# A two-layer hybrid decoder trunk: at a block's first attention step, the logits and exponentials placed ahead of the row factors' spreading and eviction

## What is computed

```python
score = sum_h relu(q_idx k_idx) * w_idx            # indexer, per query
score = where(causal, score, NEG_INF)
_, sel = top_k(score, 256)                          # 256 keys per query
logits = q k[sel] * scale + rel_bias[t5_bucket(q_pos - sel)]
logits = where(dist >= 0, logits, NEG_INF)
p = softmax(logits)                                 # 8 heads, one shared key/value head of 64
out = p v[sel]
```

## Time and profile before

| what | value |
|---|---|
| runs | 2717.36, 2715.64, 2711.79 us; median 2715.64 |
| the profiled execution | 2709.55 us, span 2707.8 us, mean granted TensorE clock 0.977 |
| TensorE busy | 2575.2 us, 95% |
| VectorE busy | 1551.7 us, 57% |
| ScalarE busy | 1019.2 us, 38% |
| GpSimd busy | 1312.4 us, 48% |
| HBM | 84 GB/s over the span |

### The profile page before, as it was taken

One profiled execution on the slowest core, in us unless ns is written; L12 is line 12 of the kernel. 1 busy time (PEld: TensorE's weight loads), 2 busy tenths in 40 slices (PEclk: granted clock), 3 DMA queues, 4 the chain that ended last, 5 costly groups with the idle time before them and its releaser, 6 DMA issues. The chain is left out here.

```text
span 2707.8 us, 34637 instructions
## 1 busy us (share of the span) xinstructions
PE 2575.2 (95%) x13515; PEld 2025.7 (75%) x13515; DVE 1551.7 (57%) x2691; ACT 1019.2 (38%) x1478; POOL 1312.4 (48%) x818
## 2 busy tenths in 40 slices
PE   8899889989999999999999999998999999999998
PEld 6667656767777777777777887766777777888887
DVE  4768777789997225844331394668899922211112
ACT  5232354233444533324344422432434354322222
POOL 3332244454454464535555532543546446655654
PEclk9989999999999999999999999999999999999999
DMA  5242113122222163323222342222222215333332
GB/s 163 72 133 58 40 57 92 51 75 65 76 76 71 51 191 87 86 63 95 85 82 82 86 129 56 81 60 63 78 65 76 71 51 184 89 97 102 101 117 86
DMA packets 385666, 232.92 MB, mean 86 GB/s; under 512 B 29592, under 2 KB 371552, under 8 KB 383072
## 3 DMA queue, kind: packets, MB, share of 16 engines
q1 hardware_dynamic: 385136, 229.62, 28.7%
q10 hardware_dynamic: 368, 1.08, 0.1%
HBM read 213.88 MB, written 14.69 MB: 84 GB/s over the span
## 5 line engine op out<-in xcount | busy, mean ns | idle before, releaser
L709 POOL TENSOR_TENSOR w_lo<-w_raw,w_hi 128x1024 fp32r<-128x1024 f32 (+2 forms) x408 | 902.2, 2212 | 1244.1 <-ACT w_hi L820 1244.1
L1744 PE MATMUL psum<-h_hi,w_hi 128*128 128x512 f32 x1984 | 799.3, 403 | 18.1 <-DVE scratch L1250 7.9
L820 ACT ACTIVATE w_hi<-w_raw 128x1024 fp32r<-128x1024 f32 (+2 forms) x408 | 397.3, 974 | 1092.7 <-PE psum L1744 1050.6
L1744 PE MATMUL psum<-h_lo,w_hi 128*128 128x512 f32 x1984 | 767.0, 393 | 0.9 <-POOL h_lo L717 0.9
L1744 PE MATMUL psum<-h_hi,w_lo 128*128 128x512 f32 x1984 | 515.1, 390 | 0.0
L1744 PEld LDWEIGHTS psum<-h_hi,w_hi 128*128 128x128 f32 x1984 | 377.0, 190 | 130.7 <-issue 35.4
L1744 PEld LDWEIGHTS psum<-h_lo,w_hi 128*128 128x128 f32 x1984 | 375.9, 190 | 79.3 <-issue 2.0
L1744 PEld LDWEIGHTS psum<-h_hi,w_lo 128*128 128x128 f32 x1984 | 373.9, 188 | 76.7
L1344 DVE MAX8 top<-scores 128x8 f32<-128x512 f32 (+5 forms) x352 | 324.0, 920 | 6.7
L1346 DVE MATCH_REPLACE8 scores<-top,scores 128x512 f32<-128x512 f32 (+5 forms) x352 | 318.8, 906 | 0.0
L1744 PE MATMUL psum<-a_hi,w_hi 128*128 128x512 f32 x704 | 286.5, 407 | 18.4 <-ACT w_hi L820 8.3
(11 more groups left out here) (310 smaller groups left out, 2946.7 us busy)
## 6 DMA issues: line engine op xcount, KB each, us to landing
w_raw<-in_w_ffn_in_dram SPq DMA_DIRECT2D x176, 512.0 KB, 3.8
w_raw<-in_w_ffn_out_dram SPq DMA_DIRECT2D x96, 384.0 KB, 3.1
w_raw<-in_w_in_dram SPq DMA_DIRECT2D x68, 512.0 KB, 3.8
w_raw<-in_w_out_dram SPq DMA_DIRECT2D x32, 512.0 KB, 3.6
x_half<-xs SPq DMA_DIRECT2D x8, 1024.0 KB, 7.0
xs<-x_half SPq DMA_DIRECT2D x8, 1024.0 KB, 6.5
w_raw<-in_w_ffn_out_dram SPq DMA_DIRECT2D x32, 256.0 KB, 2.6
out_dram<-mixed SPq DMA_DIRECT2D x8, 512.0 KB, 3.6
```

What stands on the lines that cost most here:

```text
L709: eng.tensor_tensor(w_lo(u, n), w_raw[:, u % 3, 0:n], w_hi[:, u % 2, 0:n].bitcast(F32), ALU.subtract).then_inc(sems["weights_ready"], 1)
L820: act(w_hi[:, u % 2, 0:n], w_raw[:, u % 3, 0:n], ACTF.Copy).then_inc(sems["hi_ready"], 1)
L1744: return eng.matmul(out_, lhsT, rhs, start=start, stop=stop, skip_group_check=True)
```

## The change

On both engines a call moves inside its step. On ScalarE, `row_factors` (the eviction) goes from ahead of the step's exponentials to behind them. On TensorE, `row_factors` (the spreading) goes from ahead of the step's logits to behind them. VectorE, GpSimd and SyncE keep their instructions and their order. The attention ends (`attend_end`) keep theirs too.

```diff
             def attend(l, h, b, j, s):                     # ScalarE
                 ...
-                if j == 0 and not first:
-                    row_factors(at_)
                 for n, g in enumerate(at_.banks):
                     i = 2 * j + n
                     eng.wait_ge(sems["nmax_ready"], st.add("nmax_ready"))
                     act(at_.prob[:, n, 0:nk], bank(g, 0, nk), ACTF.Exp, scale=-1.0, bias=nmax[:, i:i + 1],
                         accum_out=rsum[:, i:i + 1]).then_inc(sems["p_ready"], 1)
+                if j == 0 and not first:
+                    row_factors(at_)

             def attend(l, h, b, j, s):                     # TensorE
                 ...
                 if s == 0:
                     if not first:
                         values(at_, *((b, j - at_.pairs) if j else (b - 1, PAIRS - at_.pairs)))
-                    if j == 0 and not first:
-                        row_factors(at_)
                     ...
                     for g in at_.banks:
                         leave(g, "p_ready")
+                    if j == 0 and not first:
+                        row_factors(at_)
```

## The result

The changed kernel takes 2726.22 us in the median of its seven runs (2719.20 to 2727.68), the kernel before 2715.64 in its seven beside them: a ratio of **1.004, 95% interval 1.0028 to 1.0052**. The change costs about 10.6 us, 0.4%. The profiled execution took 2727.68 us, 18.1 more than that of before. Not all of it is the change: the attention of the first layer begins with the maxima of block 0, at 320.44 us in the trace of before, and nothing ahead of them is moved, yet there the changed kernel is already 9.6 us late. A second profile of the same kernel (the run `again`) is 1.6 us late there. So the two traces are compared from that point on, as shifts of VectorE's same instruction.

What follows compares the result with a forecast made beforehand. VectorE sets the pace through ScalarE in two stretches, TensorE elsewhere. Terms -0.94 + 5.1 + 3.0 + 0.45 = +7.6 us, giving a median of 2723.2 us; range 2713.5 to 2728, the forecast's own 2720 to 2726.

Steps and rivals of the forecast that it cites:

- Part 3, VectorE's delay: Block 6, both layers: VectorE's normalising waits 2.5 us for the late eviction and the delay reaches TensorE; +5.1 us in all.
- Part 4, the clock: Behind block 6's copies wait, grown to 3.9 us, TensorE's clock falls; 1.5 us a layer, +3.0 us in all.
- The refund at the next wait: At 821.65 TensorE's wait would shrink by what TensorE lost, so the fall there may be milder: up to 1.2 us back.
- Part 3's bound, the table load: Block 6, ScalarE: a second table load, 1.3 us a layer above the 2.5, as upper bound; not expected.
- Part 1, TensorE's half: Logits ahead of the spreading fill TensorE's 0.47 us wait for the factors at block 7; -0.94 us over two layers.
- Part 5, block 5: Block 5: normalising starts 1.7 us later, covered by 1.95 us of VectorE idle time: 0, else up to 1 us a layer.
- Part 5, the projection window: First layer's blocks 1 to 3: the late eviction delays VectorE's normalising and the next maxima; +0.45 us, bounds -0.5 and +1.2.
- Rival A: VectorE's delay is carried, but the clock doesn't fall or the fall is refunded at 821.65; +4.6 us, 2720.2; chance 0.25.
- B: Block 6: the delay isn't carried, as the copies hang on ScalarE's own order; -0.5 us, 2715.1; chance 0.10.
- C: Earlier logits shorten block 5's wait by 1.1 us and the clock stays up; 8 us faster, 2707.6; chance 0.03.
- D: Block 5's cover fails too and its delay is carried; +2 us on the forecast, 2725 to 2728; chance 0.06.

Runs made afterwards that it cites:

- act_only: The kernel before with only ScalarE's half, the eviction behind the exponentials; TensorE as before. 2720.99 us, ratio 1.003 to the kernel before.
- act_b6: The kernel before with the eviction behind the exponentials at block 6 alone, in each layer; 2723.76 us, ratio 1.0028 to the kernel before.
- deferred: The changed kernel with VectorE's normalising of the block before moved behind the next search round; 2710.30 us, ratio 0.9994 to the kernel before.
- fill: The changed kernel with unread filler products in TensorE's idle time at block 6 and at blocks 2 and 3; 2719.59 us, ratio 1.0011 to the kernel before.
- pe_only: The kernel before with only TensorE's half, logits ahead of the spreading; ScalarE as before. 2710.04 us, ratio 0.9995 to the kernel before.
- combined: The kernel before with TensorE's half everywhere, ScalarE's half with deferred normalising only in the first layer's projection window; 2716.90 us, ratio 1.0005 to the kernel before.
- maxima_first: TensorE's half everywhere, ScalarE's with deferred normalising in the projection window, block 5's four search rounds behind pair 0's maxima; 2711.87 us, ratio 0.9986 to the kernel before.
- spread: TensorE's half everywhere, ScalarE's with deferred normalising in the projection window, block 5's four search rounds spread over later steps; 2710.30 us, ratio 1.000 to the kernel before.

## Why the prediction was right, and which term was not

The forecast was 2723.2 us in 2713.5 to 2728; the median is 2726.22, 3.0 above it and inside the range, though 0.2 above the forecast's own 2720 to 2726. Against the kernel before it said +7.6 and +10.6 came. By the steps:

- **Part 3, VectorE's delay** (2 x 2.5): right, to 0.05 us. L1366 waits 2.48 and 2.47. The path was the one named: product, Silu, copies, values product. `act_only`, `act_b6` and `deferred` show that this wait and nothing else starts it.
- **Part 4, the clock** (2 x 1.5): the fall came, at an idle time of 4.46 us where 3.9 was forecast (counted from block 6's first maxima, the values product starts 2.6 us later and TensorE comes to the wait 0.5 us earlier; the 0.5 has no cause shown). Of its loss VectorE felt 2.18 us, by the row at 810.13 (forecast: 2.2 from the earlier trace rows). `fill` puts it at 2.2 by another route. The refund at the next wait came too: 2.69 instead of 3.15 us, followed by a half-clock stretch of some 3.4 us instead of 6.8, 0.9 back of the 1.2 allowed, though not for the reason given, the shorter wait (last section). Net 2.3 - 0.9 = 1.4 a layer for 1.5: right in sum, with the 0.9 open in its cause. The rule of the Trainium skill that was weighed there ("TensorE: Matmul & The Clock Gate", HAM oscillation) held at 4.46 us.
- **Part 3's bound, the table load**: ScalarE's exponential at 782.32 again starts 1.29 us after its load at 781.03, as in 60 of the 99 loads of this trace, so the 2.66 us of the Trainium skill ("ScalarE: Activation LUTs", What ACT_TABLE_LOAD costs) doesn't appear there. No second load did either: before has 99 too.
- **Part 1, TensorE's half** (-0.94): -0.78 and -0.76, so -1.5. The wait of 0.47 us is gone as said, and from the values product to the next unit it takes 4.51 us (873.45 to 877.96) for 5.22 (857.71 to 862.93). Of the rest, 0.17 us is that the next products start 0.92 us behind the spreading's start, now that they are the unit's, where the logits started 1.09 behind it; why was not looked into.
- **Part 5, block 5**: its L1366 waits 1.55 us (forecast 1.7), the two idle times behind it absorb that (0.21 us is left at 696.00), and block 6 begins unshifted (-0.05). The cover held.
- **Part 5, the projection window** (+0.45, bound +1.2): this is **the term that was mis-sized**. P costs +2.3 and +3.0 in the two profiles, and act_only +3.6. What was left out of it is TensorE's clock, which the forecast weighed at block 6 and here, without a word, put at nothing.

TensorE in time in P of the changed kernel; VectorE at block 2 and ScalarE ahead of TensorE's third row; the windows of the changed kernel, then of before. Last the place of TensorE's third row in `deferred`, and that kernel's window:

```profile
370.01 1.53 PE L1744 MATMUL psum<-xs,vw 128*64 128x128 f32 x24 [1.51 <-ACT xs L1021]
374.95 2.74 PE L2064 MATMUL psum<-cst,xs 128*128 128x128 f32 x12 [1.92 <-ACT xs L1037]
...
388.80 3.62 PE L1744 MATMUL psum<-xs,vw 128*64 128x128 f32 x32 [1.82 <-ACT xs L1021]
```

```profile
368.42 0.69 DVE L1366 TENSOR_TENSOR mixed<-psum,area 128x512 f32<-128x512 f32 x1 [1.36 <-ACT area L1025]
...
386.15 0.61 ACT L1025 ACTIVATE area<-psum 128x512 f32<-128x512 f32 x1
386.62 1.59 ACT L1021 ACTIVATE xs<-psum 128x512 f32<-128x512 f32 x3
```

```profile
374.00:382.00 8.00, 6.38 (x38) 5.05 (x40) 5.62 (x17) 3.99 (x12) 2.88 (x6) 0.57 0.00 0
388.00:394.00 6.00, 5.20 (x40) 4.00 (x40) 0.49 (x1) 0.70 (x2) 0.26 (x1) 0.72 0.00 0
```

```profile
340.00:392.00 52.00, 40.73 (x316) 28.02 (x315) 33.26 (x86) 26.26 (x73) 18.43 (x31) 1.00 0.07 22
```

```profile
377.52 1.97 PE L1750 MATMUL psum<-xs,vw 128*64 128x128 f32 x32 [1.83 <-ACT xs L1021]
```

```profile
340.00:392.00 52.00, 41.05 (x319) 28.28 (x317) 34.51 (x86) 27.25 (x76) 19.41 (x32) 1.00 0.08 24
```

Three waits of TensorE grew. L1366 of block 2 waits 1.36 us, the maxima behind it are late by it, and TensorE's wait for the next exponentials (374.95) goes from 0.89 to 1.92 us. And the eviction, at 386.15 for instance, stands between the exponentials and the copies, as the forecast said: TensorE's wait for the copies goes from 1.02 to 1.51 at block 2 and from 1.34 to 1.82 at block 3. The clock fell behind the 1.92 and the 1.82; before, the window from 340 to 392 us ran at 1.00 throughout. The forecast looked for falls only where an idle time grew toward the 3.15 us it knew. Falls between 340 us, where the moved steps begin, and 395 us, by run: changed 2, again 2, act_only 1, fill 1; none in before, pe_only, deferred, act_b6, combined, maxima_first and spread. The wait of 1.8 us for the copies is in deferred, combined, maxima_first and spread as well, and there the clock stayed at 1.00. So the falls come with the late eviction and an undeferred L1366, and never without.

This table divides P. It is worked out from the profiles: how much later than before each kernel is at four marks, counted from block 0's second maxima.

| run | block 2, second maxima (364.36) | block 3, first (372.88) | block 3, second (381.57) | end of P (390.97) |
|---|---|---|---|---|
| changed | +0.14 | +0.73 | +2.86 | +2.85 |
| again | +0.13 | +0.96 | +3.06 | +3.05 |
| act_only | +1.52 | +1.51 | +3.54 | +3.54 |
| deferred | -0.98 | -1.50 | -0.97 | -0.96 |

combined, maxima_first and spread, which defer L1366 in P too, agree with deferred to 0.04 us. That row holds what the earlier logits bring less what the evictions cost ScalarE. Against it the changed kernel loses 1.1 us at block 2 to VectorE's wait, as `again` does. At block 2, then, the forecast was near: +0.43 was said, +0.14 came. At block 3 the changed kernel loses 1.1 and 1.6 us more and `again` 1.4 and 1.6, where the clock is down, so some 2.7 to 2.9 us go with the two falls. In act_only the one fall falls on the values product of block 3, which takes 3.51 us for 1.97: of the 2.03 us lost there 1.5 are the clock and 0.5 the eviction. `fill`, without the second fall, comes out 1.3 to 1.5 us under the changed kernel's two profiles. That act_only is the latest in P with only one fall has its reason in the first column: it lacks what the earlier logits bring.

With P at its measured +2.3 to +3.0 (from its first mark) and block 7 at -1.5, the forecast's sum would have been -1.5 + 5.1 + 3.0 + 2.3 to 3.0 = 8.9 to 9.6, and the profiles show 8.95 and 9.93. Rival A (no fall) fell with the windows at 0.57, B (the delay isn't carried) with 797.18's wait of 4.02, C with block 5's wait of 4.52 us, and D with block 6's unshifted beginning. D's range did reach the result, for another reason than its own.

**Open** is why the clock fell behind 1.8 to 1.9 us of idle time in P and not at other places, nor at the same place in deferred (last section). The medians' differences, 10.6 and for `again` 10.1, exceed the 8.95 and 9.93 of the profiles by 1.6 and 0.2; the interval of the first ratio, 7.6 to 14 us, holds both.

## What to carry to other kernels

- To price a producer moved later on one engine, look first at its consumer on another: if it stands at the head of that engine's queue with work behind it that could have run, the wait counts in full wherever that engine has no idle time, and nothing where it has. Here 0.6 us moved on ScalarE became 2.5 us on VectorE, because a table load and two exponentials of 1.0 us stood between. If the order on the producer must stay, moving the consumer behind one independent piece of work takes the loss away.
- A stall of TensorE costs itself and what its clock does behind it. Here they were about equal: 2.5 and 2.2 us; a later wait came 0.9 us cheaper, for a reason that stays open. Count idle times of under 2 us as well: in P the clock cost more (2.7 us) than the wait of VectorE that came with it (1.1).
- Where an engine was busy 93 to 97% over a long stretch, moving its work about in the stretch moved the others' waits and gained nothing, in two tries. Look for its idle time first: that, and not the longest wait of the others, is the most that can be had.

## What the runs showed of the hardware beyond that

- **The length of an idle time alone didn't decide the clock.** Behind idle times of 1.82 and 1.92 us in P the granted clock was at its lower level, 1.2 GHz, for some us (windows 0.57 and 0.72). Behind 1.89 us at 680.28 (`maxima_first`; window 680 to 690), 1.94 at 784.99 (`deferred`) and 1.87 at 789.24 (`fill`) it stayed at 1.00. Behind 2.03 us at 755.16 (`spread`) it fell. Nor did the place decide: behind the same copies wait of block 3 the clock fell in changed and again (1.82 us in both) and act_only (1.82), and stayed at 1.00 in deferred, combined, maxima_first (1.83 each) and spread (1.82). In those three that fell, the wait for exponentials ahead of it was 1.92 us, in the four others 0.86 or 0.87; but behind 1.92 us itself it fell in changed, again and `fill` and not in act_only. These runs don't say what decides. A light load alone doesn't either: deferred's P, without a fall, is as light as that of before (TensorE busy 41.05 and 40.73 of 52 us, against 68.45 of 73 in the search stretch).
- **Equal idle times, unequal falls.** The fall behind 799.52 lasted some 6.8 us by windows of 2 us, that behind 838.28 some 3.4, where the same step had 6.8 before: this is the table's refund. It is not the shorter wait (2.69 for 3.15 us) that makes it so. In `fill` that step waits 3.17 us in both layers, at 825.86 and at 2138.95, and the windows behind (columns as in the earlier trace rows) differ:

```profile
825.00:833.00 8.00, 7.14 (x27) 6.35 (x28) 7.83 (x12) 2.71 (x5) 3.79 (x3) 0.59 0.10 29
2136.00:2144.00 8.00, 5.04 (x23) 4.74 (x24) 7.86 (x12) 3.09 (x5) 3.81 (x3) 0.79 0.22 66
```

  The first layer keeps the long fall (refund -0.10), the second has a short one (-1.12). So about 1 us of such a fall doesn't hang on the length of the idle time ahead of it or on the step; on what, these runs leave open. The changed kernel (both profiles), act_only and act_b6 had the refund in all eight cases, maxima_first in both, pe_only, deferred, combined and spread in none of eight. A forecast can put it in its range only.
